# Two norms between layers 1 and 2 become one root taken beside the first tile; folds, Fourier results and a split change places

## What is computed

```python
def rmsnorm(x, g):                       # rms(x, g) of the second block is the same
    return x * rsqrt(mean(x * x, axis=-1) + EPS) * g

def first_block(x, c, ctx, ...):         # layers 0 and 1
    for l in range(2):
        sh1, sc1, ga1, sh2, sc2, ga2 = split(silu(c) @ w_mod[l] + b_mod[l], 6)
        h = rmsnorm(x, g_norm1[l]) * (1 + sc1) + sh1
        pf, mq, mk, mv, mo, mg, cq, ckv, kr = split_proj(h @ w_in[l])
        y_f = fft2(pf).real              # over tokens and within groups of 64 features
        y_m = mlstm(...); y_a = attention(...)
        x = x + ga1 * (concat(y_f, y_m, y_a) @ w_out[l])
        h2 = rmsnorm(x, g_norm2[l]) * (1 + sc2) + sh2
        x = x + ga2 * (relu(h2 @ w_up[l]) ** 2 @ w_down[l])
    return rmsnorm(x, g_final)           # the final norm, between layers 1 and 2

def second_block(x, c, ...):             # layers 2 and 3
    for l in range(2):
        sh1, sc1, gt1, sh2, sc2, gt2 = split(silu(c) @ w_ada[l] + b_ada[l], 6)
        h = rms(x, g_mix[l]) * (1 + sc1) + sh1
        parts = split(h @ w_in[l])       # queries, keys, values, dilated groups, two gates
        mixed = sigmoid(parts[12]) * y_a + sigmoid(parts[13]) * y_b
        x = x + gt1 * (mixed @ w_out[l])
        h2 = rms(x, g_mlp[l]) * (1 + sc2) + sh2
        x = x + gt2 * (relu(h2 @ w_ff1[l]) ** 2 @ w_ff2[l])
    return x
```

## Time and profile before

| | |
|---|---|
| median of three runs | 3662.9 us (3669.1, 3656.46, 3662.9) |
| the profiled execution | 3666.42 us |
| its span in the profile | 3664.6 us |
| mean granted clock of TensorE | 0.978 |
| TensorE products (PE) | 3491.9 us busy, 95% |
| TensorE weight loads (PEld) | 2742.0 us, 75% |
| VectorE | 2131.2 us, 58% |
| ScalarE | 1225.1 us, 33% |
| GpSimd | 310.6 us, 8% |

### The profile page before, as it was taken

One profiled execution on the slowest core, in us unless ns is written; L12 is line 12 of the kernel. 1 busy time (PEld: TensorE's weight loads), 2 busy tenths in 40 slices (PEclk: granted clock), 3 DMA queues, 4 the chain that ended last, 5 costly groups with the idle time before them and its releaser, 6 DMA issues.

```text
span 3664.6 us, 45096 instructions
## 1 busy us (share of the span) xinstructions
PE 3491.9 (95%) x17152; PEld 2742.0 (75%) x17152; DVE 2131.2 (58%) x2847; ACT 1225.1 (33%) x1516; POOL 310.6 (8%) x320
## 2 busy tenths in 40 slices
PE   7998999999998898899997999999999999999999
PEld 3676868888887676678885577778887567778887
DVE  6456557646667465576666565267667665355343
ACT  1235444122113245342223333333223443333222
POOL 0000102001001000010000010001011000001000
PEclk9999999999999998999998999999999999999999
DMA  8221202322332121034441011225443111222222
GB/s 335 76 76 52 73 2 91 127 92 92 117 112 77 53 79 70 24 129 168 163 163 62 31 66 57 81 104 186 165 165 115 49 53 58 73 100 93 102 92 103
DMA packets 52252, 359.58 MB, mean 98 GB/s; under 512 B 5960, under 2 KB 6600, under 8 KB 11024
## 3 DMA queue, kind: packets, MB, share of 16 engines
q1 hardware_dynamic: 35744, 256.92, 19.9%
q10 hardware_dynamic: 16368, 100.73, 7.5%
HBM read 355.31 MB, written 2.32 MB: 98 GB/s over the span
## 4 chain that ended last, share of the span: by engine, by line
PE 52%; issue 32%; DVE 10%; ACT 4%; DMA 1%; POOL 1%; DVEq 0%; ACTq 0%; POOLq 0%
PE pair L540 21%; PE pair L1036 10%; PE pair L607 3%; PE pair L1106 2%; PE pair L552 1%; PE pair L578 1%; DVE arena L2196 1%; PE pair L653 1%; PE pair L710 1%; DVE w_lo L2111 1%; PE pair L869 1%; PE pair L958 1%; ACT w_hi L1396 1%; PE pair L1181 1%; PE pair L933 1%
## 5 line engine op out<-in xcount | busy, mean ns | idle before, releaser
L2111 DVE TENSOR_TENSOR w_lo<-raw,w_hi 128x2048 fp32r<-128x2048 f32 x221 | 506.4, 2291 | 266.2 <-ACT w_hi L1396 259.7
L1396 ACT ACTIVATE w_hi<-raw 128x2048 fp32r<-128x2048 f32 x221 | 421.5, 1907 | 642.7 <-PE pair L540 589.7
L540 PE MATMUL pair<-h_hi,w_hi 128*128 128x512 f32 (+2 forms) x1856 | 601.6, 366 | 5.7 <-DVEq L2093 2.7
L540 PE MATMUL pair<-h_hi,w_lo 128*128 128x512 f32 (+2 forms) x1856 | 598.8, 365 | 0.0
L540 PE MATMUL pair<-h_lo,w_hi 128*128 128x512 f32 (+2 forms) x1856 | 598.1, 364 | 0.0
L540 PE MATMUL pair<-u_hi,w_hi 128*128 128x512 f32 (+3 forms) x1152 | 387.0, 372 | 24.5 <-DVE x L2152 13.1
L540 PE MATMUL pair<-u_hi,w_lo 128*128 128x512 f32 (+3 forms) x1152 | 384.4, 370 | 0.0
L540 PE MATMUL pair<-u_lo,w_hi 128*128 128x512 f32 (+3 forms) x1152 | 384.3, 370 | 0.0
L2196 DVE SCALAR_TENSOR_TENSOR arena<-arena,cact 128x256 f32<-128x256 f32 x756 | 369.7, 512 | 19.5
L2347 DVE TENSOR_TENSOR u_lo<-arena,u_hi 128x512 fp32r<-128x512 f32 (+1 forms) x128 | 97.1, 759 | 459.9 <-POOL arena L2875 455.0
L540 PEld LDWEIGHTS pair<-h_hi,w_hi 128*128 128x128 f32 (+2 forms) x1856 | 311.9, 184 | 68.7 <-issue 7.3
(11 more groups left out here) (352 smaller groups left out, 4919.9 us busy)
## 6 DMA issues: line engine op xcount, KB each, us to landing
raw<-in_wt_dram SPq DMA_DIRECT2D x222, 1024.0 KB, 4.8
arena<-in_modw_dram ACTq DMA_DIRECT2D x78, 1024.0 KB, 5.0
arena<-in_modw_dram SPq DMA_DIRECT2D x18, 1024.0 KB, 7.5
arena<-negm_rows_dram ACTq DMA_DIRECT2D x16, 384.0 KB, 4.0
arena<-in_fconst_dram ACTq DMA_DIRECT2D x2, 2688.0 KB, 10.1
x<-in_xt_dram SPq DMA_DIRECT2D x1, 3072.0 KB, 16.5
arena<-in_brope_dram ACTq DMA_DIRECT2D x4, 640.0 KB, 3.9
out_dram<-x SPq DMA_DIRECT2D x1, 2048.0 KB, 7.2
```

Source lines behind the costliest of these rows:

```text
L540: mm = pe.matmul(pp[p][0:m, lo:hi], a[0:rows, k * width + c0:k * width + c0 + m], b[0:rows, k, lo:hi], start=(k == 0 and i == 0), stop=(k ...
L1396: act.activation(w_hi[slot][:], raw[slot][:], ACT.Copy).then_inc(w_hi_done, 1)
L2111: dve.tensor_tensor(w_lo[slot][:], raw[slot][:], w_hi[slot][:].bitcast(F32), ALU.subtract)\
```

## The change

The two plain norms between layers 1 and 2 go, with a barrier each. Layer 2 now starts in the raw form. With final gain g and the root r1 of layer 1's output, the input of layer 2 is x g r1, and its own root r2 is that of the mean of (x g)^2 r1^2, so ScalarE squares both x and x g (`n_sq`, `n_sq2`), GpSimd sums both, TensorE makes both sums, and ScalarE and VectorE work out r1 r2 = exp(-0.5 (ln a + ln(b/a/D + eps))) with a the mean of the squares of x plus eps and b the sum of the squares of x g. The gain of layer 2 is multiplied by g (`set_half(..., final)`). x itself is multiplied by g and r1 later, in layer 2's `gqa`, two chunks after each pair of heads. Besides: the folds of the last MLP group stand one hidden tile earlier on VectorE (layers 0 to 2), and fold 0 of the first group stands before the fourth `u_lo` instead of behind it; TensorE's fold products are spread over the last down tile, fold by fold. In layer 1 the Fourier results are taken at chunk 3 instead of 5, and copied to `f_v` at once. In layers 2 and 3 the split of the gates' fourth tile stands before `high(0)` / `low(0)` of the last pair in `dilated`. The second half of the mod vector of layer 2 is made behind the first norm.

```diff
-N_PHASES = 1 + 4 + 3 + 1 + 1 + 1
+N_PHASES = 1 + 4 + 3 + 1
@@ areas
+        n_sq2 = [area(6 * T_ALL + i * S, S) for i in range(2)]
+        n_acc2 = area(6 * T_ALL + 2 * S, S)
+        first_root = x[:, 0:2, S:T_ALL]
+        def sum_products(places, double=False):
+            out = [(pp[p][:, at:at + b - a], n_acc[:, a:b], n_sq[1][:, a:b]) for p, at, a, b in places]
+            return out + ([(pp[2][:, S:2 * S], n_acc2, n_sq2[1])] if double else [])
@@ TensorE, raw_first_jobs
                     if k == 1:
-                        pe.wait_ge(acc_ready, t.next(acc_ready))
                         take_pair(sum_pair)
                         take_pair(shift_pair)
-                        for p, at, a, b in sums:
-                            pe.matmul(pp[p][:, at:at + b - a], ones[:], n_acc[:, a:b], start=True, stop=False)
+                    if k == (3 if double else 1):
+                        pe.wait_ge(acc_ready, t.next(acc_ready))
+                        for out, acc, _ in sums:
+                            pe.matmul(out, ones[:], acc, start=True, stop=False)
                         pe.wait_ge(last_sq, t.next(last_sq))
...
@@ TensorE, mlp_group
                         feature_job(w, 4, P, c * P, P, 512, U, n, (4 * half + c + 1) % 3,
                                     tile_used if c == 3 else job_dve)
-                        if last and layer < 3 and half and c == 0:
-                            folds()
-                if layer < 3 and not last:
-                    folds()
+                        if half and c < 2:
+                            folds((1, 2) if last and c else (c,))
+                if not last:
+                    folds((2,))
@@ TensorE, gqa and the program
-                if layer == 3:
-                    raw_first_jobs(tile(), (bank(0), bank(1)), S, False, tail_places(S), 2, (job_dve, tile_used))
-                else:
-                    first_jobs(tile(), (bank(0), bank(1)), S, (job_act, tile_used))
+                raw_first_jobs(tile(), (bank(0), bank(1)), S, False, tail_places(S), 2, (job_dve, tile_used), layer == 2)
...
-            norm(S)
             for layer in range(2, 4):
-                if layer == 2:
-                    norm(S)
                 gqa(layer)
@@ ScalarE, raw_square
                 act.wait_ge(sq_free, t.next(sq_free))
+                if double:
+                    act.activation(n_sq2[j % 2], x[:, j, 0:S], ACT.Square, scale=gfin[:, j:j + 1])
                 act.activation(n_sq[j % 2][:, 0:n], x[:, j, 0:n], ACT.Square).then_inc(act_pool if j < KC - 1 else last_sq, 1)
@@ ScalarE, raw_norm, behind the logarithm
+                if double:
+                    act.activation(n_r[:, 0:S], r[:, 0:S], ACT.Exp, scale=-1.0).then_inc(act_dve, 1)
+                    act.activation(first_root, halves(r[:, 0:S]), ACT.Exp, scale=-0.5)
+                    act.wait_ge(dve_act, t.next(dve_act))
+                    act.activation(n_r[:, 0:S], n_r[:, 0:S], ACT.Ln, bias=eps[:, 0:1], scale=1.0 / D).then_inc(act_dve, 1)
+                    act.wait_ge(dve_act, t.next(dve_act))
                 act.activation(r[:, 0:n], r[:, 0:n], ACT.Exp, scale=-0.5).then_inc(act_dve, 1)
...
-                    if first and j == 5:
+                    if first and j == (3 if n > S else 5):
                         first()
@@ ScalarE, dilated, last pair; gates
                         probs(1, 3, 0)
+                        split()
                         high(0)
...
-                    if i > 1:
+                    if i > 2:
                         split()
@@ VectorE, set_half (final: layer 1), raw_norm
+                if final:
+                    finish(ins)
+                    dve.tensor_tensor(gain[:, which], gain[:, which], gfin[:].unsqueeze(2).to_broadcast([P, 8, 2]), ALU.mult)
...
                 split()
+                if double:
+                    heard()
+                    finish(dve.tensor_tensor(n_r[:, 0:S], pp[2][:, S:2 * S], n_r[:, 0:S], ALU.mult), dve_act)
+                    heard()
+                    finish(dve.tensor_tensor(r[:, 0:S], r[:, 0:S], n_r[:, 0:S], ALU.add), dve_act)
                 heard()
@@ VectorE, first_features; fourier has lost these copies for layer 1
+                values_read(NT)
+            def values_read(nt):
+                for i in range(nt):
+                    job()
+                    dve.tensor_copy(f_v[:, i, :], pp[i % 2][:, 0:512]).then_inc(pair_free[i % 2], 1)
@@ VectorE, group of the MLP
                         for c in range(2):
-                            if half and c == 0 and not first and not last:
+                            if half and c == (1 if first else 0) and not last:
                                 ring_fold(0)
...
-                            if last and layer < 3 and 2 * half + c:
-                                if half == 0:
-                                    next_half_mod()
-                                ring_fold(2 * half + c - 1)
-                    if first:
-                        ring_fold(0)
+                            if last and layer < 3 and 2 * half + c < 3:
+                                if 2 * half + c == 0:
+                                    next_half_mod(layer)
+                                ring_fold(2 * half + c)
...
-                if layer == 1:
-                    second_half_mod()
@@ VectorE, gqa, behind the reciprocal and the low part of each pair of heads
+                    for c in (2 * j, 2 * j + 1) if layer == 2 else ():
+                        finish(dve.scalar_tensor_tensor(halves(x[:, c, 0:S]), halves(x[:, c, 0:S]), gfin[:, c:c + 1],
+                                                        first_root, ALU.mult, ALU.mult))
@@ VectorE, dilated, last pair; gates
                         by_key(3, 0)
+                        split()
                         low(0)
...
-                for i in range(6):
+                for i in range(5):
                     split()
@@ VectorE, the program
-            norm(S)
             for layer in range(2, 4):
-                if layer == 2:
-                    norm(S, 0, fresh=True)
-                else:
-                    raw_norm(S, 0, late_r, late_t, first_rope)
-                    second_half_mod()
+                raw_norm(S, 0, late_r, late_t, first_rope, layer == 2)
+                second_half_mod()
@@ GpSimd, add_squares
-                    if j == 0:
-                        ins = pool.tensor_copy(n_acc[:, 0:n], n_sq[0][:, 0:n])
-                    else:
-                        ins = pool.tensor_tensor(n_acc[:, 0:n], n_acc[:, 0:n], n_sq[j % 2][:, 0:n], ALU.add)
+                    for acc, sq in ((n_acc[:, 0:n], n_sq[j % 2][:, 0:n]), (n_acc2, n_sq2[j % 2]))[:2 if double else 1]:
+                        ins = pool.tensor_copy(acc, sq) if j == 0 else pool.tensor_tensor(acc, acc, sq, ALU.add)
```

## The result

The changed kernel takes 3608.4 us (median of four runs, 3599.8 to 3618.5) against 3664.8 for the kernel before (four runs): ratio 0.985, 95% interval 0.9817 to 0.9883. The medians differ by 56 us, 43 to 67 by the interval; the forecast was 3613, 50 us less. The profiled execution took 3599.83 us, its span is 3598.0, and the mean granted clock 0.988 instead of 0.978. This execution is the fastest of its four, and that of before lay above its median, so the two spans differ by 66.6 us, 10 more than the medians do.

The account below looks back on a forecast made before the run. TensorE was taken as the bound, busy 3491.9 of 3664.6 us, with stalls and clock losses to recover. Five places, 13.2 + 10.3 + 9.0 + 13.4 + 3.7 = 49.6 us off 3666.4, less 3.5 for the median: 3613, range 3603 to 3626.

Parts of the forecast that it names:

- Place 1: From layer 1 to layer 2: removing two barriers with a norm each gains 13.2 us, after a longer root chain.
- GpSimd's share: Start of layer 2: contention of GpSimd's added additions with VectorE costs 0.5 us, bounds nothing and 3.5.
- Rival B: End of layer 1: double-root chain later by 3 us, TensorE idles 12 us instead of 8; 3617 to 3620, chance 0.13.
- Place 2: MLP ends, layers 0 to 2: earlier folds remove stalls before the fourth down product and their clock losses, 10.3 us gained.
- Place 3: Fourier results of layer 1: earlier features and copies shorten stalls and keep the clock up, 9.0 us gained.
- Place 4: Layers 2 and 3: an earlier weight split removes the stall before the gates and its clock loss, 13.4 us gained.
- Place 5: First MLP groups, layers 0 to 2: first fold moved before the fourth u_lo, 3.7 us gained.
- rival A: Moved waits return beside their old places, so MLP ends, gates and first groups give half of 27.4: 3627 us, chance 0.14.
- The threshold: TensorE's clock: stalls of 2.2 us and more bring the lower level, 1.2 GHz; those of 2.0 and less don't.
- TensorE's moved fold products: Inner MLP groups: the third fold's slack falls from 1.5 to 1.0 us; effect on time nothing.

Follow-up runs that it names:

- half_fold: Changed kernel with the fold ahead of the fourth u_lo cut in two, in first and last MLP groups of layers 0 to 2: 3609.0 us, ratio 0.9843.
- after: First trace of the changed kernel, nothing else altered: profiled execution 3599.83 us, the fastest of four runs with median 3608.4 us.
- last_folds_old: Changed kernel with VectorE's folds of the last MLP groups one hidden tile later, as originally: last-group stretches 98.3, 111.7, 99.2 us instead of 95.1, 107.7, 96.3.
- before: The kernel without the change, in its first trace: median of four runs 3664.8 us.
- before_again: The kernel without the change, run and traced once more: 3662.4 us.
- after_again: The changed kernel run and traced once more, as the measure for other runs: 3612.8 us, ratio 0.9851.

## Why the prediction was right, point by point

- **The bound and the reading.** TensorE's stalls and the clock behind them carried the result: idle time fell by 38 us, busy time by 29. The total of 50 us against 56 measured is right, but it owes some of this to terms that miss on either side, which is luck.
- **Place 1, 13.2 us.** By the traces 14.4 (90.2 less 75.7 from the first fold product). Of the steps, the rope product was forecast 9.5 us later than in layer 3 and came 9.5 later (37.3 against 27.8); the chain from the logarithm to VectorE's first chunk took 4.45 us where I had 5.0; the idle time was 7.3, forecast some 8. The clock behind it cost 1.4 us (38.4 against 37.05 us from the rope product to the values), where I took 2.5 to 2.6 from a stall of 4.46. In the other traces with a stall of 7.3 it cost up to 2.7 (half_fold), so my 2.6 was the upper end of it. The windows show why: the clock falls while the stall still lasts, and only the low part behind it costs anything. In after (first three lines) it is low from 1956.4, 4 us before the rope product, to 1963.2, 2.8 us behind its start; in half_fold (fourth) it stays low for 5.5 us behind the start. Half of that is the price.

```profile
1956.40:1960.40 4.00, 0.00 (x1) 0.03 (x1) 2.73 (x7) 1.68 (x3) 0.79 (x1) 0.50 0.00 0
1960.40:1963.20 2.80, 2.80 (x5) 1.25 (x5) 1.09 (x2) 2.28 (x4) 1.75 (x2) 0.50 0.00 0
1963.20:1968.00 4.80, 4.80 (x22) 3.77 (x21) 4.42 (x9) 3.74 (x4) 0.00 (x0) 1.00 0.00 0
1965.98:1971.50 5.52, 5.52 (x9) 3.07 (x10) 3.67 (x7) 4.54 (x8) 1.72 (x2) 0.50 0.00 0
```

- **GpSimd's share, 0.5 us.** VectorE's low parts took 1.1 to 1.5 us instead of 0.7 beside the additions of some 1.4 us, but taking six additions away let TensorE's rope product start only 0.9 us sooner. Rival B's 12 us of idle time did not come. The Trainium skill (SBUF — State Buffer, "Who interferes with whom") has the two exclude each other for the whole instruction. The durations don't contradict this, but each lost 0.4 to 0.8 us, part of an addition's length, and the path of this kernel did not pay the 3 us that I had worked out from it.
- **Place 2, 10.3 us.** 10.1 by last_folds_old. By the table it is 13.4; of the 3.3 more, 1.6 in layer 2 is the clock, which fell behind the stall there in both traces of before and not in last_folds_old, and 1.6 in layer 0 is the mean of what the clock cost behind two blocks of fold products there, 3.1 in before_again and nothing in before. The stall before the fourth u_lo grew by 0.9 in sum (6.0 to 6.8 us, means of two traces), forecast 1.3.
- **Place 3, 9.0 us.** 11.5 by the table: 4.1 for the stall, as forecast (3.9), and 7.5 behind it, where I had 2.7 + 0.7 + 1.7, 5.1. The mis-sized term is the slow clock in the first products: I compared the 3.75 us of the first eight with the 3.09 of the second as if these were at full speed. Both were slow, the second but for the start; the sixteen take 3.88 us at full clock, 3.0 less, not 0.7.
- **Place 4, 13.4 us.** 12.4 (5.8 and 6.6, means of two traces each). The stalls went entirely.
- **Place 5, 3.7 us.** This step failed: by the table the first groups gained 0.4 in layer 0 and 0.5 in layer 1 and lost 1.6 in layer 2, nothing in sum or a little less than that. The loss in layer 2 is the clock, which fell behind the new stall in both traces of the changed kernel and not behind the old one. The stalls before the fourth slice are 2.3 us in all three layers, forecast 2.0 and 1.2. In layer 0 the fold takes twice as long, and I let the wait shrink because the products ahead are longer too, without walking that queue as I did for layer 1. Here rival A was right, in this place alone: a fold of 4 us moved from behind a deadline to before one costs what it cost. half_fold shows that half of the fold fits on either side, with 0.7 us of stall left.
- **The threshold.** That the clock stands at its lower level behind stalls of 2.2 us and more, and not behind those of 2.0 and less, is wrong as a rule, and the trace that it was read from already spoke against it: the stalls of 2.20 and 2.21 us in the first groups of layers 0 and 2 were not followed by the lower clock there (windows of before, first fence below), only that of layer 1 was. The same stall of 2.45 us at the end of layer 1's mix left the clock at 1.00 in after and at 0.50 in after_again, 2.8 us apart (windows, 5.5 us from its end, second and third fence). Over all 14 traces, from 100 us on, the lower clock began in or up to 3.5 us behind 53 of 125 stalls of 1.9 to 2.3 us and 63 of 75 of 2.3 to 2.8 us; places with other stalls close by are not sorted out. The longer, the likelier, with no threshold between 2.0 and 2.2.

```profile
637.00:641.00 4.00, 3.90 (x22) 3.42 (x23) 3.89 (x11) 0.00 (x0) 0.00 (x0) 1.00 0.72 266
2500.50:2504.50 4.00, 4.00 (x18) 3.31 (x19) 3.78 (x8) 0.88 (x1) 0.00 (x0) 1.00 0.73 262
```

```profile
1544.30:1550.00 5.70, 5.67 (x25) 4.70 (x26) 4.01 (x7) 3.36 (x6) 2.22 (x3) 1.00 0.01 1
```

```profile
1555.50:1561.00 5.50, 5.50 (x13) 4.34 (x14) 3.26 (x6) 2.62 (x5) 1.57 (x2) 0.50 0.00 1
```

- **What was missed.** In the inner groups I put "nothing" for TensorE's moved fold products. They gave some 7.4 us in layer 0 and cost 1.4 in layers 1 and 2, so 6 net: more than I gave place 5, from an edit without any wait. This and 2.5 more at place 3 make up for place 5.

The places by the measurements are 14.4 + 10.1 + 11.5 + 12.4 + 0 and 6 for the spread fold products, 54 us; the medians give 56. The table's numbers rest on two traces of each kernel, in which chance has a part of a few us.

## What to carry to other kernels

Price an edit to the tensor engine's queue by what it does to the granted clock too: here a run of 24 tiny products of 2.73 us was followed by the lower clock in 18 of 28 places without the engine ever being idle, and spreading it was worth more than its own time. A block of work that must pass a deadline is often better cut in two around it than moved from one side to the other. Where one execution spreads by more than the edit is worth, compare stretches between fixed products over several traces, and take two traces of the same kernel before a difference is given a cause.

## What was not expected of the hardware

- Behind 18 of 28 blocks of 24 products with one output column (2.73 us, no idle time) the clock fell to its lower level for some 3 us, 1.55 us lost; behind none of 70 groups with blocks of eight (0.95 us).
- The clock behind one and the same stall of 2.45 us fell in one execution and not in another.
- At clock 1.00 layer 0's pairs of 512 and 256 columns run at one of two paces, 69.26 or 70.5 us a group, in the same program.
- What the lower clock costs behind a stall does not grow with the stall: behind 7.3 us of idle time 1.4 us in after and 2.7 in half_fold, behind 4.46 us 2.5. The clock falls within a long stall, and half of the low stretch that is left when it ends, 2.8 and 5.5 us in the first two, is the price.
